# Transposing the mixer output and two residual norms by DMA instead of on the TensorE

## The reference, cut to what matters

```python
h = rmsnorm(x, g_mix)                       # (B, S, 1024)
q, k, v, g, u, sv = split(h @ w_in)         # 6 x 512 columns
r = chunk_retention(rotary(q), rotary(k) * 128**-0.5, v)     # 4 heads of 128
y_ret = silu(g) * layernorm_nogain(r) * ret_norm_g
y_sg  = spatial_gating(gelu(u), gelu(sv), w_s, b_s, sg_norm_g)
x = x + concatenate([y_ret, y_sg]) @ w_out                   # mixer output
x = x + square(relu(rmsnorm(x, g_ffn) @ w_ff1)) @ w_ff2      # first residual norm
x = x + sigmoid(rmsnorm(x, g_ple) @ w_ple_gate) * (p @ w_ple)  # second residual norm
return rmsnorm(x, g_final)
```

## Time and profile before

| | |
|---|---|
| median of 3 runs | 3312.07 us (3306.49 to 3314.06) |
| the profiled execution | 3312.35 us; span of its slowest core 3310.8 us |
| spans of the eight cores | 3299.4 to 3310.8 us |
| busy share: TensorE, VectorE, ScalarE, GpSimd | 94%, 57%, 35%, 20% |
| DMA engines, mean busy share | 56.8% (queue of the kernel's own DMAs) |

### The profile page before, as it was taken

One profiled execution on the slowest core, in us unless ns is written; L12 is line 12 of the kernel. 1 busy time (PEld: TensorE's weight loads), 2 busy tenths in 40 slices (PEclk: granted clock), 3 DMA queues, 4 the chain that ended last, 5 costly groups with the idle time before them and its releaser, 6 DMA issues.

```text
span 3310.8 us, 48382 instructions; the slowest of 8 cores (3299.4 to 3310.8 us)
## 1 busy us (share of the span) xinstructions
PE 3121.7 (94%) x16270; PEld 1503.4 (45%) x16592; DVE 1898.4 (57%) x3842; ACT 1143.4 (35%) x1792; POOL 660.0 (20%) x605
## 2 busy tenths in 40 slices
PE   3697699999999999999999999999999999999998
PEld 1343244444444444444444444444444444444444
DVE  3573275565747556474665647556574755647444
ACT  2544442333324233332323333233332423333233
POOL 1240031231302213031131302113130221312101
PEclk9798899999999999999999999999999999999999
DMA  8888985564635546464564646446474555645442
GB/s 266 255 275 252 294 265 178 180 216 165 229 144 183 209 172 216 159 227 156 188 202 157 232 150 214 181 166 216 166 229 153 189 193 184 222 144 196 147 153 102
DMA packets 118466, 647.66 MB, mean 196 GB/s; under 512 B 13648, under 2 KB 13904, under 8 KB 64976
## 3 DMA queue, kind: packets, MB, share of 16 engines
q1 hardware_dynamic: 118224, 644.55, 56.8%
HBM read 583.68 MB, written 60.82 MB: 195 GB/s over the span
## 4 chain that ended last, share of the span: by engine, by line
PE 90%; DMA 4%; DVE 2%; issue 2%; ACT 1%; SPq 1%; POOL 0%; DVEq 0%; ACTq 0%; POOLq 0%
PE ps L617 85%; DMA stage<-wf 3%; PE ps L625 3%; DMA stage<-xT 1%; SPq L503 1%; PE ps L925 0%; PE ps L757 0%; PE ps L793 0%; PE ps L805 0%; PE ps L795 0%; ACT ringF L584 0%; ACT rel L1020 0%; DMA stage<-pT 0%; ACT scr L916 0%; DVE TG L873 0%
## 5 line engine op out<-in xcount | busy, mean ns | idle before, releaser
L617 PE MATMUL ps<-ringM,TG 128*128 128x512 bf16 x3996 | 955.1, 381 | 23.8 <-ACT rel L1020 8.7
L617 PE MATMUL ps<-TG,ringF 128*128 128x512 bf16 x4007 | 938.5, 380 | 25.3 <-ACT scr L916 8.5
L617 PE MATMUL ps<-ringF,hT 128*128 128x512 bf16 x3996 | 918.5, 382 | 44.8 <-ACT ringF L584 35.9
L1023 DVE TENSOR_TENSOR hT<-rel 128x512 bf16<-128x512 f32 x486 | 403.3, 830 | 408.7 <-ACT rel L1020 404.7
L617 PEld LDWEIGHTS ps<-ringF,hT 128*128 128x128 bf16 x4096 | 395.8, 98 | 493.4 <-issue 54.7
L617 PEld LDWEIGHTS ps<-TG,ringF 128*128 128x128 bf16 x4096 | 396.7, 98 | 487.3 <-issue 31.5
L617 PEld LDWEIGHTS ps<-ringM,TG 128*128 128x128 bf16 x4096 | 396.7, 98 | 480.2 <-issue 30.9
L1020 ACT ACTIVATE rel<-ps 128x512 f32<-128x512 f32 x512 | 304.5, 595 | 692.8 <-PE ps L617 686.9
L713 POOL TENSOR_TENSOR qk<-scr 128x512 bf16<-128x512 f32 x128 | 164.2, 1283 | 1459.1 <-DVE scr L710 1459.1
L1040 DVE SCALAR_TENSOR_TENSOR xb<-ps,st,xb 128x512 f32<-128x512 f32 x256 | 191.0, 748 | 410.0 <-PE ps L617 409.7
L632 ACT ACTIVATE xsb<-xb 128x1024 bf16<-128x1024 f32 x192 | 202.1, 1053 | 423.3 <-DVE xb L1040 300.6
(11 more groups left out here) (85 smaller groups left out, 2518.8 us busy)
## 6 DMA issues: line engine op xcount, KB each, us to landing
ringF<-wb SPq DMA_DIRECT2D x240, 1024.0 KB, 6.0
ringM<-wb SPq DMA_DIRECT2D x150, 1024.0 KB, 6.2
stage<-wf SPq DMA_DIRECT2D x104, 512.0 KB, 8.1
stage<-xT SPq DMA_DIRECT2D x64, 512.0 KB, 5.9
xb<-x SPq DMA_DIRECT2D x64, 512.0 KB, 5.7
stage<-x SPq DMA_DIRECT2D x64, 512.0 KB, 10.1
out<-xb SPq DMA_DIRECT2D x64, 512.0 KB, 6.4
wb<-ringF SPq DMA_DIRECT2D x16, 1024.0 KB, 11.2
```

Of the source, the lines that this page charges most:

```text
L617: r = e.matmul(out(), lhs(k), rhs(k), start=(start + k == 0), stop=(start + k == total - 1))
L1023: fsq = lambda e, r=r, o=o: e.tensor_tensor(out=ap(o), in0=ap(r), in1=ap(r), op=ALU.mult)
```

## The change

`dmaT` is a new helper that enters one operation for ScalarE's queue: a DMA transpose from SBUF to SBUF. `yT` calls it for its 128x512 bf16 piece (131072 bytes) and `norm_T` for its 128x1024 piece (262144 bytes). The transposes on the TensorE, their PSUM banks and the copies out of them are gone in these two places. Transposes of the keys (`X2`, line 743) stay on the TensorE. Line numbers of the changed kernel differ by up to 6.

```diff
--- before.py
+++ after.py
@@ -626,6 +626,11 @@
                 return r
             return {"pe": (n * MS, fn)}
 
+        def dmaT(out, in_, reads, writes, vt, key, nbytes):
+
+            g.add({"act": (0.2, lambda e: e.dma_start_transpose(out=out(), in_=in_()))}, reads, writes, vt, dma=key,
+                  nbytes=nbytes)
+
         def sqsum(xbuf, acc, racc, vt):
 
             j = g.buf("xsb")
@@ -865,14 +870,8 @@
             ymix = g.buf("TG")
 
             def yT(b, half, src):
-                p = g.buf("psum")
-                g.add(transposes(p, lambda k: ap(src)[:, k * 128:(k + 1) * 128], 4), [(src, 0), c("ident")], [(p, 0)],
-                      vt[0])
-                o_ = lambda: ap(ymix)[:, 4 * half:4 * half + 4, b * 128:(b + 1) * 128]
-                i_ = lambda: psb(p)[:, 0:512].rearrange("p (k n) -> p k n", k=4)
-                g.add(both(512, lambda e: e.tensor_copy(out=o_(), in_=i_()),
-                           lambda e: e.activation(out=o_(), in_=i_(), func=AF.Copy), mode=2),
-                      [(p, 0)], [(ymix, (half, b))], vt[0])
+                dmaT(lambda: ap(ymix)[:, 4 * half:4 * half + 4, b * 128:(b + 1) * 128], lambda: ap(src), [(src, 0)],
+                     [(ymix, (half, b))], vt[0], lambda: ("ty", src.slot), 131072)
                 adv(4 * MS)
 
             X2(0)
@@ -991,13 +990,8 @@
             g.add(both(1024, lambda e: e.tensor_copy(out=ap(xs), in_=ap(xx)),
                        lambda e: e.activation(out=ap(xs), in_=ap(xx), func=AF.Copy)),
                   [(xx, 0), (xx, 1)], [(xs, 0)], vt, lock=("dve",))
-            p = g.buf("psum")
-            g.add(transposes(p, lambda k: ap(xs)[:, k * 128:(k + 1) * 128], 8), [(xs, 0), c("ident")], [(p, 0)], vt)
-            o_ = lambda: ap(dst)[:, :, b * 128:(b + 1) * 128]
-            i_ = lambda: psb(p).rearrange("p (k n) -> p k n", k=8)
-            g.add(both(1024, lambda e: e.tensor_copy(out=o_(), in_=i_()),
-                       lambda e: e.activation(out=o_(), in_=i_(), func=AF.Copy)),
-                  [(p, 0)], [(dst, b)], vt)
+            dmaT(lambda: ap(dst)[:, :, b * 128:(b + 1) * 128], lambda: ap(xs), [(xs, 0)], [(dst, b)], vt,
+                 lambda: ("tx", xs.slot), 262144)
 
         def ffn(t):
             vt = [t * TILE]
```

## The result

The changed kernel is slower: 3344.3 and 3349.1 us against 3306.5 to 3314.1 us before, a ratio of 1.0108 with a 95% interval of 1.0083 to 1.0132.

The account below looks back on a forecast made before the run. The TensorE was taken as the bound in the long middle, not in the first 400 us: 3312.35 - 87 + 8 + 15 + 4 = 3252 us, with a range of 3222 to 3400 us.

Parts of the forecast that it names:

- the one on waits: ScalarE and TensorE waiting for transposed pieces: covered by 6.9 us of free PSUM banks; 1 us for each of 15 tiles.
- L = 5 us: Time from issue to landing of a 256 KB norm piece, taken as 5 us between 2.0 and 11.3.
- the burst of six issues: Six mixer pieces issued in a row on ScalarE before the MLP's ReLUs: 3 us, covered by about 6.9 us, cost nothing.
- The removal (-87 us): TensorE transposes of 128 norm and 128 mixer pieces taken away, at 0.45 and 0.23 us of its queue: 87 us.
- the lower bound only: Low end of the range, 3221 or 3222 us, which alone counted 8.8 us of TensorE waits on PSUM copies as saved.
- not returned: Removed TensorE transposes in the first 400 us, where it waits for weights anyway: 8 us of the saving not gained.
- Issuing: 256 DMA transposes on ScalarE's queue: 1.0 us a norm piece, 0.5 us a mixer piece, 192 us replacing 93; no bound.
- The condition: At the six mixer pieces on ScalarE: an issue of over 1.1 us would make the burst show on the TensorE.
- mark for "right": Sign that the forecast holds: waits of ScalarE's Squares on DMA transposes stay under 7 us a piece.
- The first rival: ScalarE stands behind late landings at both norms: at 11.3 us each, 10.5 us per tile, 158 us, 3395 us; chance 0.27.
- the deciding 0.93: Rival that the DMA engines become the bound: decides at 0.93 us of all 16 per 128x128 block; chance 0.05.
- The end (+4 us): At the last tile's gate nothing is left to hide the landing of norm pieces behind: 4 us added.

Follow-up runs that it names:

- e6: Changed kernel, same order, with all 256 DMA transposes issued from SyncE in place of ScalarE: 3209.4 to 3210.0 us, ratio 0.9688.
- e1: Changed kernel, same order, with every one of the 256 DMA transposes made a ScalarE copy, so nothing is transposed there: 3202.27 us, one execution.
- e10: Changed kernel, transposes still on ScalarE, but from the third tile on each weight ring load moves an eighth of its bytes: 3267.7 to 3303.7 us, ratio 0.9898.
- e7: Against e6: idle ScalarE copies added at each transpose's place in the changed kernel's order, two per mixer piece, three per norm piece: 3223.5 and 3226.7 us.
- e2: Changed kernel, same order and queue, with each DMA transpose made a plain DMA of the same 256-byte rows: 3233.4 to 3240.6 us, ratio 0.9775.

## Why the prediction was wrong

The step that failed is the one on waits. Every landing was taken at L = 5 us and held covered, the burst of six issues too, and 15 us were left for what remained; the first 400 us were put at no cost. Against the same transposes on SyncE's queue (e6) the runs show, in the middle, 74 us more idle time of the TensorE and 19 us more at a lower clock, and 43 us at the start.

The account of the slowest cores, changed kernel against e6. e6's rows of the third and last tile mark:

```profile
586.79 0.18 DVE L985 RECIPROCAL st<-st 128x4 f32<-128x4 f32 x1
...
3025.05 0.18 DVE L985 RECIPROCAL st<-st 128x4 f32<-128x4 f32 x1
```

First three tiles 629.5 - 586.8 = 43 us; next thirteen 2531.2 - 2438.3 = 93 us; the end -1 us. Together 134 us before rounding, against 3344.3 - 3209.9 = 134. Of the 93, 74 are more idle time of the TensorE (75.7 against 1.5 us): 42 for late norm pieces, 25 for the GELU behind the burst, the rest for other things. The other 19 are longer busy time (2455.5 against 2436.7 us), at a granted clock of 0.99 against 1.00.

- **The removal (-87 us) was right,** and the waits that went with it were worth more than allowed. e1 gains 110 us: its TensorE is busy for 76 us less than before (3045.6 against 3121.7), and the idle time in the middle fell from 46 us to 6; I had put 8.8 us of that into the lower bound only (which comes to 3220.6, not 3221 or 3222). In the changed kernel the busy time fell by 40 us and not by the 80 to 90 that were to show, since part of it ran at the lower clock.
- **The first 400 us, counted only as 8 us that are "not returned", were a failed step.** I had seen 83 to 88% busy DMA engines there and took it only as a place where nothing is gained. That much was right: with nothing by DMA (e1) the first three tiles take 576 us on the median over the cores, and 578 before. But it is a place where transposes on a second queue cost: they take 616 us in the changed kernel, 38 more, and 49 more on the slowest cores. More transfers alone are not the cause: e6 moves the same pieces there in 577 us.
- **Issuing was mis-sized.** 1.0 and 0.5 us were taken; 1.30 and 1.35 us are the medians, and the mixer pieces in a burst take 1.7 each. The bound from above, ScalarE's own copy of 0.60 us, was no bound for a mixer piece. The condition, "if an issue took over 1.1 us, the burst would show on the TensorE", named the right place but too low a price: with bursts of 9.6 to 10.4 us it shows, 27 us from 400 to 3200 us; with bursts of 7.7 us (e10) or 7.5 us of copies (e7), 1.25 us a piece and more, no such wait shows.
- **Landing: the middle value was near, the use of one value was the main failure.** L = 5 us stands against medians of 6.3 and 6.6. But no tile stalls at the median. In the stall shown two pieces of 24 and 27 us stand in a chain through `xsb`, where a run of ring loads is in flight; four waits of this kind make up the 42 us. Those waits were in the working (the Squares behind d33 and d34) and I held them covered. ScalarE stood for 175 us in 30 such waits, up to 34.9, where the text's own mark for "right" was under 7 us a piece. (In e6 it stood for 108 us in 37 of them, none over 8.7 us, and the TensorE waited for none of its norm pieces in the middle.)
- **The argument against the rival was turned round.** I wrote that "the transposes have a queue of their own instead of standing behind other loads". e6 shows that on SyncE's queue, among the loads, the tail stays short. The first rival, ScalarE standing behind late landings, was thus true in part: late norm pieces are 42 us of idle time, and the burst and the start were not in it. Its price, 83 us above no change, was too high, because it took L = 11.3 for every piece.
- **The DMA engines did not become the bound.** 12.0% of 3342.8 us are 401 us for 1,536 blocks, 0.26 us a block, against the deciding 0.93. The Trainium skill's 1309 ns (VectorE: DVE Perf Modes, "The three transpose paths"), taken as occupation, is five times above this trace.
- **The end (+4 us)** was too much: in the last tile the TensorE waits 0.54 us for a norm piece.
- **One core was not enough.** The prediction worked on one core; with rare stalls, the slowest of eight is what counts.

Not separated: within the 93 us of the middle, how much is ScalarE held by a long issue (in the stall shown two took 7.56 us together) and how much the landing itself. Both grow in the same places. In e6 the long issues stay but hold SyncE, and after the first 400 us no norm piece on core 1 takes over 15.1 us to land; in e10 both are mostly gone in the middle. Why a transpose beside loads of another queue is so much worse than a plain copy there stays open.

## What to carry to other kernels

Before moving work to DMAs, ask which queue it will be on and what is in flight beside it: against the same kernel with nothing transposed, these 256 transposes cost 142 us on ScalarE's separate queue and 8 us on the queue of the weight loads, and plain copies of the same rows on the separate queue 35. Price a new transfer by its late tenth in the crowded places and by the buffers that wait for it, not by a median; and with several cores, by the slowest of them. An issue is work of the engine that makes it; a burst of issues needs the cover of its whole length.

## What the runs showed of the hardware that was not expected

- Two queues that are busy together delay each other's transfers unevenly: after the first 400 us, one in ten of the 256 KB transposes beside 1 MB loads of another queue took over 15.1 us to land (core 1; at most 27.1), and over 4.6 us where these loads were cut to an eighth (e10, core 5). The loads' own packets took the DMA engines 119 us more in all than before (59.8% of 3342.8 us against 56.8% of 3310.8), for the same bytes. The Trainium skill (DMA: Bandwidth & Descriptors, "Queues, rings and completion order") says that each DMA engine goes round robin between the queues it has work for, a packet at a time; by that, a small piece beside a long load would get a part of each engine instead of standing behind the load. That landings are longer beside loads agrees with it; that the tail is shorter on the loads' own queue (8.6 us in e6) does not follow from it. No run here shows the packets' order.
- A transpose is dearer than a plain copy of the same rows: 12.0% of 3342.8 us against 7.5% of e2's 3231.8 us, 401 against 242 us of the DMA engines (321 us in e10 beside lighter loads, 9.8% of 3275.1), and an issue of 1.30 us against 0.60 for a norm piece. The Trainium skill (Advanced Engine Details and Errata, "X-Bar Transpose (TRN2)") has transposes as fast as regular DMAs; in this kernel, with pieces of 128 and 256 KB inside SBUF, they are not.
- An issue is not of fixed length: 1.2 to 7.1 us for a norm piece on ScalarE, up to 11.0 on SyncE. It grows with the loads beside it: after the first 400 us one in ten took over 4.3 us in the changed kernel (core 1), over 1.3 in e10 (core 5).
